# Side modulation weights issued from GpSimd's queue in a float32 two-network transformer kernel on one Trainium2 core

## The reference, cut to what matters

```python
def modulation(cvec, w_mod, b_mod):
    m = (jax.nn.silu(cvec) @ w_mod + b_mod).reshape(-1, 1, N_MOD * D_MODEL)
    return jnp.split(m, N_MOD, axis=-1)
```

```python
x = x + g2 * sq_relu_mlp(modulate(rms_norm(x, norm2_g[l]), sh2, sc2), w_mlp1[l], w_mlp2[l])
```

## Time and profile before

| what | value |
|---|---|
| median of 3 runs | 4267.09 us |
| the profiled execution, its own time | 4267.01 us |
| span of its instructions | 4265.2 us |
| TensorE busy | 3649.4 us (86%) |
| VectorE busy | 1925.8 us (45%) |
| ScalarE busy | 1389.0 us (33%) |
| GpSimd busy | 0.9 us, 8 instructions |
| DMA | 359.49 MB, 27.2% of 16 engines' span on the queue used by SP |
| mean granted TensorE clock | 0.923 of full |

### The profile page before, as it was taken

The page is one execution under the profiler, slowest core; times in us unless marked ns, Lnnn a source line. Parts: engine busy times, 40 slices in busy tenths (PEclk is TensorE's granted clock), DMA queues, the critical chain, the costliest instruction groups (busy, mean ns, idle before and its releaser), DMA issues. The chain is left out here.

```text
span 4265.2 us, 43758 instructions
## 1 busy us (share of the span) xinstructions
PE 3649.4 (86%) x18105; PEld 2926.8 (69%) x18105; DVE 1925.8 (45%) x2972; ACT 1389.0 (33%) x1912; POOL 0.9 (0%) x8
## 2 busy tenths in 40 slices
PE   8496478899999967778899599879987999977998
PEld 3473254688888735448777477768876888867887
DVE  0214434445555433446676455543344545553333
ACT  1310224443223412335222444442233323334223
POOL 0000000000000000000000000000000000000000
PEclk9797689999999978889999799989998999988999
DMA  7211100123333211014665122112322323221321
GB/s 239 80 41 53 41 27 1 50 93 110 114 114 104 60 73 41 6 40 154 202 222 192 44 69 60 60 65 93 99 75 66 80 67 88 62 79 60 99 98 50
DMA packets 411199, 359.49 MB, mean 84 GB/s; under 512 B 58570, under 2 KB 405593, under 8 KB 409851
## 3 DMA queue, kind: packets, MB, share of 16 engines
q1 hardware_dynamic: 411003, 356.72, 27.2%
HBM read 351.39 MB, written 2.10 MB: 83 GB/s over the span
## 5 line engine op out<-in xcount | busy, mean ns | idle before, releaser
L675 PE MATMUL ps<-second_h_hi,second_w_hi 128*128 128x512 f32 (+1 forms) x1776 | 684.6, 385 | 78.1 <-DVE second_h_lo L897 49.5
L675 PE MATMUL ps<-second_h_lo,second_w_hi 128*128 128x512 f32 (+1 forms) x1776 | 665.8, 375 | 0.0
L675 PE MATMUL ps<-second_h_hi,second_w_lo 128*128 128x512 f32 (+1 forms) x1776 | 665.6, 375 | 0.0
L747 DVE TENSOR_TENSOR second_w_lo<-ring,second_w_hi 128x2048 fp32r<-128x2048 f32 (+2 forms) x140 | 290.7, 2077 | 438.6 <-ACT second_w_hi L699 438.6
L675 PE MATMUL ps<-h_mix_hi,w_hi 128*128 128x512 f32 (+1 forms) x1192 | 423.2, 355 | 49.4 <-DVE h_mix_lo L897 25.6
L675 PEld LDWEIGHTS ps<-second_h_hi,second_w_hi 128*128 128x128 f32 x1776 | 346.7, 195 | 138.9 <-issue 56.4
L675 PE MATMUL ps<-h_mix_lo,w_hi 128*128 128x512 f32 (+1 forms) x1192 | 418.0, 351 | 0.0
L675 PE MATMUL ps<-h_mix_hi,w_lo 128*128 128x512 f32 (+1 forms) x1192 | 416.8, 350 | 0.0
L675 PEld LDWEIGHTS ps<-second_h_lo,second_w_hi 128*128 128x128 f32 x1776 | 346.9, 195 | 55.9 <-issue 1.7
L675 PEld LDWEIGHTS ps<-second_h_hi,second_w_lo 128*128 128x128 f32 x1776 | 344.8, 194 | 57.9
L699 ACT ACTIVATE second_w_hi<-ring 128x2048 fp32r<-128x2048 f32 (+2 forms) x140 | 242.8, 1735 | 240.8 <-PE ps L675 230.1
(11 more groups left out here) (364 smaller groups left out, 5578.3 us busy)
## 6 DMA issues: line engine op xcount, KB each, us to landing
ring<-in_w_mlp SPq DMA_DIRECT2D x64, 1024.0 KB, 5.4
side_w<-in_ada_w SPq DMA_DIRECT2D x96, 512.0 KB, 4.9
ring<-in_ffn_w_in SPq DMA_DIRECT2D x44, 1024.0 KB, 5.0
wm<-in_w_mod SPq DMA_DIRECT2D x24, 1024.0 KB, 10.3
side_w<-in_w_mod SPq DMA_DIRECT2D x48, 512.0 KB, 3.7
ring<-in_attn_w_in SPq DMA_DIRECT2D x48, 512.0 KB, 5.3
ring<-in_hgrn_w_in SPq DMA_DIRECT2D x32, 512.0 KB, 5.4
ring<-in_ffn_w_out SPq DMA_DIRECT2D x16, 1024.0 KB, 5.2
```

The source lines that it names most:

```text
L675: mm = pe.matmul(acc, lhsT, rhs, start=k == 0 and wp == ap, stop=k == j.kt - 1 and wp == 1)
L747: dve.tensor_tensor(unit.place(unit.slot[1]), unit.place(M.ring[:, u % RING, :]), unit.place(unit.slot[0]), ALU.subtract).then_inc(*S.w_lo ...
```

## The change

`SideThread`'s issuing generator is moved from SP to GpSimd, and gets a wait at its start; `Thread` gets an empty GpSimd generator for all the other threads; `Region.emit` writes out a GpSimd block, in all four regions of the program.

```diff
@@ class Thread
+    def gpsimd(self, pool):
+        yield from ()
@@ Region.emit
+            @block.gpsimd
+            def _(pool):
+                weave((), [s.gpsimd(pool) for s in self.sides])
@@ class SideThread
-    def sync(self, sp):
+    def gpsimd(self, pool):
         S, n = self.S, len(self.columns)
+        pool.wait_ge(S["block_lo"].sem, S["block_lo"].at(KD))
         for u in range(self.UNITS):
             for half, r in enumerate((slice(0, KD // 2), slice(KD // 2, KD))):
                 yield self.start + (u - 1) * self.pitch + (half + 1) * self.pitch / 2
                 if u and half:
-                    sp.wait_ge(S.side_acc.sem, S.side_acc.at(u))
+                    pool.wait_ge(S.side_acc.sem, S.side_acc.at(u))
                 elif u:
-                    sp.wait_ge(S.side_step.sem, S.side_step.at(((u - 1) * (KD - 1) + KD // 2) * n))
+                    pool.wait_ge(S.side_step.sem, S.side_step.at(((u - 1) * (KD - 1) + KD // 2) * n))
                 for t, side in enumerate(self.sides):
                     piece = cut(side.w, 0, D, u * UNIT).src
-                    sp.dma_start(self.sw[:, t, r, :], piece[:, r, :]).then_inc(*S.side[half].one)
+                    pool.dma_start(self.sw[:, t, r, :], piece[:, r, :]).then_inc(*S.side[half].one)
```

## The result

| | before | after |
|---|---|---|
| median | 4269.25 us (6 runs) | 4287.97 us (6 runs, 4284.77 to 4297.81) |
| ratio, 95% interval | | 1.0048, 1.0034 to 1.0062 |
| span of the profiled execution | 4265.2 us | 4287.1 us |

Both kernels were timed side by side here, so the median of before is not quite the one at the top. The ratio is estimated from all twelve runs; the quotient of the two medians alone is 1.0044, or 18.7 us, and lies in the same interval. The forecast was 4301 us, slower; the direction and the place were right, the size was too large.

What follows compares the result with a forecast made beforehand. In layer 1's stage TensorE runs right behind VectorE, which waits 21.4 us for side weights; layer 0's TensorE is always busy. Only layer 1 costs: 40 x 0.5 x 1.7 = 34 us on 4267.09 gives 4301 us, range 4262 to 4385.

Steps and rivals of the forecast that it cites:

- d = 2 us: Both side-work stages: a side half lands this much later when GpSimd issues it; bounded between 0 and 5.4 us.
- Main fetches, SP's issue time, the blocks at the stages' ends: 0 us: Earlier main fetches are hidden, SP's saved issue time is idle time, GpSimd's four blocks add nothing: 0 us each.
- Layer 1, 40 x 0.5 x 1.7 = 34 us: Layer 1's stage: VectorE's added waiting, times the share reaching TensorE, times the clock's loss, makes the kernel 34 us slower.
- 40 us more waiting on VectorE: Layer 1: 16 reloads already waited for grow, 32 us; five others add some 1.5 us each.
- Half passes on: Layer 1: half of VectorE's added waiting reaches TensorE, 20 us of stall; idle time of VectorE absorbs the rest.
- The place I had named for a wait that passes: Layer 1: VectorE's 2.74 us wait before 2218.34, 1.3 us ahead of a store (L1082) that TensorE was said to await.
- Times 1.7 for the clock: Layer 1's TensorE: 21 us lost to low clock beside 31 us of stalls, so 1.7 us per us of stall.
- The expected view: Landing 6 to 8 us, layer 1 longer by 25 to 50, side waits about 60, TensorE's at L1044 about 50.
- A, no difference: Both side-work stages: landing under 0.6 us later, or VectorE's idle time absorbs nearly all; 4267 to 4275 us, chance 0.22.
- B, GpSimd's pace: Layer 1: each transfer holds GpSimd over 3.7 us, so it sets the unit's time; 112 us more, 4379, chance 0.20.
- C, VectorE holding GpSimd up: Transfers wait up to 2.29 us, twice a half, for VectorE's two-input instructions; +90 us, 4357, chance 0.06.
- D, faster: Side halves on their own queue no longer stand behind main units, VectorE waits less; 18 us gained, 4249, chance 0.07.

## Why the prediction was right, and where its size was off

**d = 2 us** held: 2.0, by luck in good part, since its reasons held only for the smaller share. I had put it down to GpSimd's pace in making a list. Of the 2.0 us the later start and slower issue are 0.6. The other 1.4 are a longer landing; about 0.3 of that layer 0's transfers show too, and the rest is met in the 16 reloads that now have a main fetch ahead of them. In all the others the second DMA lands no later than before (5.6 us against 5.7), so d is no constant of a GpSimd transfer.

**Layer 0, 0 us**: held (1.0002). The tightest reload waits 1.6 us where 1.3 were expected, and is absorbed.

**Main fetches, SP's issue time, the blocks at the stages' ends: 0 us** held for what they were costed for: no high part waits for `ring`. That an earlier main fetch delays the side's half behind it was not costed, and it is most of d. Putting the main fetches back to their old times lost more, since they then went out with the side's.

**Layer 1, 40 x 0.5 x 1.7 = 34 us**: measured about 18. By its three terms:
- *40 us more waiting on VectorE* was the first step that failed: 25.6 us (47.0 - 21.4). I took all 16 waits to grow and five to be added. By my count over the trace, which finds 18 waits before, twelve grew, by 0.6 to 2.8 us and 24.7 in all; three new ones came, of 0.3, 0.6 and 1.9 us; and six went to nothing (0.1 to 1.0 us each before). Five of these six are first halves, and before each of them a second half had just waited 2.2 to 4.4 us: the wait for a second half stands between the release of the next first half and its use, so VectorE comes later and does not wait again. In four of the five the time from release to use grew, by 1.4 to 2.6 us; and all five land sooner than before, by 0.9 to 3.7 us. A delay is not charged once for each reload.
- *Half passes on* held as a number: 14.0 us of TensorE's idle time against 25.6 is 0.55. It is a mean over unlike cases, and no constant: it was 5.0 of 21.4 for the waits of before. VectorE's waits for second halves grew by 13.5 us, and three of TensorE's waits, each at a sum within 2 us behind such a wait, from 2.16, 1.33 and 2.51 us to 5.84, 5.70 and 6.09: 11.6 of the 14.0 us. The waits for first halves grew by 12.0 us and leave 2.4. Where one stands ahead of idle time of VectorE's own, nothing passes: the wait before 2070.59 grew from 1.39 to 4.09 us, and TensorE's wait at the sum behind it stayed at 4.01. One of each kind, before and after:

```profile
2168.60 1.05 PE L1044 MATMUL ps<-ones,f 128*128 128x1 f32 x8 [1.33 <-DVE mods L1082]
2181.00 1.87 PE L1052 MATMUL ps<-ones,f 128*128 128x1 f32 x8 [5.70 <-DVE mods L1090]
```
```profile
2081.55 1.05 PE L1044 MATMUL ps<-ones,side_a 128*128 128x1 f32 x8 [4.01 <-DVE mods L1082]
2090.77 1.76 PE L1052 MATMUL ps<-ones,side_a 128*128 128x1 f32 x8 [4.02 <-DVE mods L1090]
```

  The place I had named for a wait that passes was misread. In the kernel before TensorE waits for nothing between 2195 and 2236 us, so the store at 2219.67 held nobody up. After the change it passes nearly nothing, first VectorE, then TensorE:

```profile
2236.05 0.61 DVE L1070 TENSOR_SCALAR side_a<-side_w,cond 128x256 f32<-128x256 f32 x2 [5.46 <-DMA side_w<-in_ada_w]
2236.59 0.87 DVE L1073 SCALAR_TENSOR_TENSOR side_a<-side_w,cond,side_a 128x256 f32<-128x256 f32 x2
2237.38 0.22 DVE L1090 TENSOR_TENSOR mods<-ps,vec 128x2 f32<-128x2 f32 x2
```
```profile
2237.65 1.05 PE L1052 MATMUL ps<-ones,f 128*128 128x1 f32 x8 [0.33 <-DVE mods L1090]
```

  The wait went from 2.74 to 5.46 us and TensorE idles 0.33.
- *Times 1.7 for the clock* was the second step that failed: the stage lost 18 us for 14.0 of idle, 1.29. I had set all of the stage's low clock against all of its stalls. TensorE's waits at the sum are 14 now and were 13: stalls got longer more than they got more. The clock's record has eight stretches at 1.2 GHz in the stage before and nine after, 41 and 55 us in all, and TensorE is busy in 38 us of them before and in 45 after. So 14.0 us more of stall brought 7 us more work at half speed, about 3.5 us lost (the busy time grew by 4.0), where 0.7 of 14.0 had been counted, 9.8 us.

With the two put right, 25.6 x 0.55 x 1.29 = 18 us; these are the measured terms, so the product tests nothing new.

**The expected view**: landing 6 to 8 us was too long as a median (5.4), right for the reloads that are waited for. The stage was to be 25 to 50 us longer (18), VectorE's side waits about 60 (47), TensorE's at its sum about 50 (43.5).

**The rivals.** A, no difference, fell with the interval, which begins at 1.0034. B, GpSimd's pace: a DMA holds it for 0.75 us, more than the 0.5 read from a memset and far from the 3.7 that B needs; four in a unit are 3 of 14.9 us. C, VectorE holding GpSimd up: issue follows the release by 0.30 us, in all reloads alike, and VectorE's busy time is unchanged; a DMA takes GpSimd 748 ns, shortest and median alike, whatever VectorE does. With the rule of the Trainium skill, "SBUF — State Buffer", section "Who interferes with whom", by which there would be no hold, this agrees. D, faster: landing grew. Its premise was misread as well: no side reload of layer 1 went out less than 2.3 us behind a main fetch before the change, and the 2.74 us of rows 11 were waited for a reload that had one 0.96 us behind it. The estimated sum by the first-byte figures of the Trainium skill, "DMA: Bandwidth & Descriptors", section "Latency and other measured facts", was 5 us. Its difference of 0.4 us between the two issuers is near what layer 0 shows (0.3), where little else moves; it leaves out what the transfer meets in a stage with the DMA engines at 0.6 and over, which is most of d.

Open: why a GpSimd transfer beside SP's takes 7.1 us, whether by its packets, its queue or its order of service. That it is met beside main fetches is seen in four traces; no run takes the main fetches away.

## What to carry to other kernels

Before a transfer is moved to another queue, ask what order the old queue gave it: here SP's queue served the urgent half ahead of the megabyte that nobody awaited, and a queue of its own put both side by side, or the megabyte ahead. What a late buffer needs is time between its release and its use; smaller pieces gave it that with no new queue, and made the choice of the queue nearly irrelevant. And when a delay is summed over many waits, the first ones push the waiting engine back and spare it the next: count the chain, not the reloads.

## Not expected of the hardware

GpSimd's DMAs go out in fewer, larger packets: 20736 for 144 transfers, 144 each and 3.6 KB on average, where SP's queue had 411003 in all before and 334971 without them, 528 each. The transfers were no faster for it. A DMA of GpSimd costs 748 ns at 512 KB and still 722 at 256 KB, so not by its pieces. It starts 0.30 us after a release by VectorE, SP's 0.03 us.
